# A two-layer trunk in split float32: other steps for the block sums, earlier splits of the x sums, and products of ones while x loads

## The reference, cut to what matters

```python
h = rmsnorm(x, a_norm); proj = h @ a_w_in            # 2048 x 5120
xb, gate = proj[..., :2560], proj[..., 2560:]
xb = causal_depthwise_conv(xb, ...)                  # width 4
y = rg_lru(xb, ...)                                  # two 256-wide block-diagonal products, sigmoid, scan over time
x = x + (y * silu(gate)) @ a_w_out                   # 2560 x 2048
kv = rmsnorm(x, kv_norm) @ w_kv                      # 2048 x 4096: K, then V
q, gate = split(rmsnorm(x, b_norm) @ b_w_in)         # 2048 x 4096
o = stick_breaking_attention(q, k, v)                # 16 heads of 128
x = x + (o * silu(gate)) @ b_w_out
return rmsnorm(x, final_norm)
```

## Time and profile before

| | |
|---|---|
| time, median of 3 runs | 1689.11 us (1686.1, 1689.88, 1689.11) |
| time of the profiled execution | 1688.68 us |
| its span, from the first to the last instruction | 1687.0 us |
| PE busy | 1665.7 us, 99% |
| DVE, ACT, POOL busy | 60%, 49%, 15% |
| DMA queue of SP | 216.16 MB, 41.2% of 16 engines |

### The profile page before, as it was taken

How to read it: one execution, slowest core, us unless ns; L and a number is a source line. 1 busy time by engine, 2 the same in 40 slices (tenths; PEclk the granted TensorE clock), 3 DMA queues, 4 the chain that set the end, 5 groups by cost and what they waited for, 6 DMA issues and landing times.

```text
span 1687.0 us, 24029 instructions
## 1 busy us (share of the span) xinstructions
PE 1665.7 (99%) x7743; PEld 1388.5 (82%) x7743; DVE 1017.3 (60%) x1780; ACT 818.2 (49%) x1626; POOL 260.1 (15%) x251
## 2 busy tenths in 40 slices
PE   8999999999999999999999999999999999999998
PEld 6888888877888888878888888888888888888888
DVE  5787787778774544476664556465655647463333
ACT  6555566655565333355655535444454545432223
POOL 0121211121221313220002111111111111113100
PEclk9999999999999999999999999999999999999999
DMA  5555555665533232346765332323233232323223
GB/s 184 174 180 165 185 168 171 198 196 166 154 95 99 97 97 96 96 146 192 228 189 159 98 100 82 100 81 93 82 105 93 81 100 82 100 76 119 94 94 132
DMA packets 179606, 216.95 MB, mean 129 GB/s; under 512 B 12808, under 2 KB 137944, under 8 KB 179416
## 3 DMA queue, kind: packets, MB, share of 16 engines
q1 hardware_dynamic: 179544, 216.16, 41.2%
HBM read 190.95 MB, written 25.17 MB: 128 GB/s over the span
## 4 chain that ended last, share of the span: by engine, by line
PE 77%; DVE 8%; ACT 5%; DMA 5%; issue 4%; SPq 1%; DVEq 0%; ACTq 0%; POOL 0%; POOLq 0%
PE ps L544 74%; DMA b_raw<-in_w_kv 2%; DVE w_lo L1176 2%; DMA t_scratch<-b_raw 2%; DVE b_raw L1335 1%; PE ps L711 1%; ACT w_hi L817 1%; DVE w_lo L1174 1%; DVE rbuf L1313 1%; ACT w_hi L819 1%; DMA stage<-in_a_w_in 1%; ACT abuf L899 1%; ACT L899 1%; ACT tbuf L896 1%; DVE tbuf L1309 1%
## 5 line engine op out<-in xcount | busy, mean ns | idle before, releaser
L544 PE MATMUL ps<-x_hi,w_hi 128*128 128x512 f32 x1408 | 552.6, 392 | 0.1
L544 PE MATMUL ps<-x_hi,w_lo 128*128 128x512 f32 x1408 | 549.1, 390 | 0.0
L544 PE MATMUL ps<-x_lo,w_hi 128*128 128x512 f32 x1408 | 548.9, 390 | 0.0
L1174 DVE SCALAR_TENSOR_TENSOR w_lo<-stage,cT,w_hi 128x256 fp32r<-128x256 f32 x352 | 206.3, 586 | 329.2 <-ACT w_hi L819 328.8
L817 ACT ACTIVATE w_hi<-stage,cT 128x256 fp32r<-128x256 f32 x352 | 178.4, 507 | 320.1 <-PE ps L544 315.1
L544 PEld LDWEIGHTS ps<-x_hi,w_hi 128*128 128x128 f32 x1408 | 265.0, 188 | 56.9 <-DVE w_lo L1176 3.0
L544 PEld LDWEIGHTS ps<-x_hi,w_lo 128*128 128x128 f32 x1408 | 264.7, 188 | 55.3
L544 PEld LDWEIGHTS ps<-x_lo,w_hi 128*128 128x128 f32 x1408 | 264.9, 188 | 53.6 <-issue 0.2
L1171 DVE TENSOR_TENSOR w_lo<-stage,w_hi 128x512 fp32r<-128x512 f32 x160 | 128.2, 806 | 214.2 <-ACT w_hi L815 214.2
L815 ACT ACTIVATE w_hi<-stage 128x512 fp32r<-128x512 f32 x160 | 100.4, 630 | 279.9 <-PE ps L544 260.0
L819 ACT ACTIVATE w_hi<-stage,cT 128x256 fp32r<-128x256 f32 x352 | 174.4, 496 | 0.0
(11 more groups left out here) (202 smaller groups left out, 2278.8 us busy)
## 6 DMA issues: line engine op xcount, KB each, us to landing
stage<-in_a_w_in SPq DMA_DIRECT2D x160, 256.0 KB, 2.9
stage<-in_b_w_in SPq DMA_DIRECT2D x128, 256.0 KB, 2.8
stage<-in_w_kv SPq DMA_DIRECT2D x95, 256.0 KB, 2.8
stage<-in_a_w_out SPq DMA_DIRECT2D x80, 256.0 KB, 2.6
b_raw<-in_w_kv SPq DMA_DIRECT2D x64, 256.0 KB, 3.5
t_scratch<-b_raw SPq DMA_DIRECT2D x64, 256.0 KB, 3.3
stage<-in_b_w_out SPq DMA_DIRECT2D x64, 256.0 KB, 2.6
stage<-t_scratch SPq DMA_DIRECT2D x45, 256.0 KB, 3.2
```

Of the source, the lines that this page charges most:

```text
L544: mm = pe.matmul(dst, a, b, start=start and n == 0, stop=stop and n == 2, skip_group_check=not check)
L1174: nc.vector.scalar_tensor_tensor(w_lo[:, slot, 0:256], stage[:, slot, 0:256], cT[:, col:col + 1], f(w_hi[:, slot, 0:256]), ALU.mult, ALU.s ...
```

## The change

Three things are changed.

1. **Weight sums.** `b_raw` becomes two sets (c even, c odd), each with its own counters, and the steps change: `T_IN`, `T_OUT` and `T_SUM` are now lists. DVE makes the two groups of an 18-step block at steps 4, 5, 6, 7, 10 and 11, 13, 16, 16, 17.
2. **x sums.** Six of the eight S2 tiles are now split in the last iteration of stage 2. The split of the last two residual tiles (`work2` at position 22) moves behind V step 9 on DVE. POOL makes its last x sums only when DVE has split the operands of 9 V steps, and adds its last squares only after 32.
3. **Start.** PE multiplies `ones` by `ones` (128x128, float32) 4 times before it turns the norm's row, 5 times behind it, and 3 times behind the first transposes. Unit 0 is cut in two: its half with column tile 0 stands ahead of the transposes of tiles 2 and 3, the half with tile 1 behind them. ACT does one small activation on `ones` first, so that its table is loaded before the first weights arrive.

```diff
-S2_HI_AT = {2: 4, 3: 5, 4: 7, 5: 9, 6: 11, 7: 13}
-S3_HI_AT = {i: 8 + 2 * i for i in range(VP)}
+S2_HI_AT = {6: 10, 7: 12}
+S3_HI_AT = {i: 8 + 2 * i if i else 9 for i in range(VP)}
...
-T_IN, T_SUM, T_OUT = 16, 3, 24
+T_IN, T_OUT = (16, 18, 34, 36), (27, 35, 45, 53)
+T_SUM = {4: (0,), 5: (1,), 6: (2,), 7: (3,), 10: (4,), 11: (5,), 13: (6,), 16: (7, 8), 17: (9,)}
...
-                b_raw = sb("b_raw", [P, 4, 512], F32, mem_b)
+                b_raw0 = sb("b_raw0", [P, 4, 512], F32, mem_b)
+                gap("below_b_raw1", 2 * (KR - 4) * 1024, mem_b)
+                b_raw1 = sb("b_raw1", [P, 4, 512], F32, mem_b)
...
-                if not isinstance(it, int) or 4 * it + c:
-                    sp.wait_ge(t_out, it * 256 + 64 * c)
+                if not isinstance(it, int) or 2 * it + c // 2:
+                    sp.wait_ge(t_out[c % 2], it * 128 + 64 * (c // 2))
...
                     for at_j, step in ((T_OUT, sums_out), (T_IN, blocks_in)):
-                        n, e = divmod(9 * c + at_j, N1)
+                        n, e = divmod(at_j[c], N1)
...
+            def spin(times):
+
+                for _ in range(times):
+                    pe.matmul(ps[2][:, 0:P], ones[:, :], ones[:, :], start=True, stop=True)
+
+            pe.wait_ge(id_made, 2)
+            spin(4)
             pe.wait_ge(id_made, 3)
             pe.wait_ge(gain_in, 16)
             turn_rows(rows_g, GAIN_ROWS).then_inc(rows_turned, 1)
+            spin(5)
             turn_x(0)
-            for j in range(8):
+            spin(3)
+            pe.wait_ge(x_lo_ready, 1)
+            unit_t(0, U1, 0, x_hi, x_lo, 0, KD, (0,))
+            turn_x(2)
+            pe.wait_ge(x_lo_ready, 2)
+            unit_t(0, U1, 0, x_hi, x_lo, 0, KD, (1,))
+            for j in range(1, 8):
                 if j < 7:
                     turn_x(2 * j + 2)
...
+            act.wait_ge(id_made, 2)
+            nc.scalar.activation(rb[:, 0:P], ones[:, :], ACT.Identity)
             act.wait_ge(table_ready, 1)
             hi(1, 0, U1)
...
-                    if last and q in (2, 3):
-                        sum_hi(S2, q - 2)
+                    if last and q < 6:
+                        sum_hi(S2, q)
...
-                    if not last and T_SUM <= q % 9 < T_SUM + 5:
-                        block_sum(it, q // 9, q % 9 - T_SUM)
+                    if not last and q % 18 in T_SUM:
+                        for n in T_SUM[q % 18]:
+                            block_sum(it, 2 * (q // 18) + n // 5, n % 5)
...
-                    if last and q in (3, 4):
-                        sum_lo(S2, q - 3)
+                    if last and 1 <= q < 7:
+                        sum_lo(S2, q - 1)
                     if last and LOOK <= q < LOOK + 4:
                         value_step(q - LOOK)
-                    work2(it, q + LOOK)
+                    if not last or q + LOOK != 22:
+                        work2(it, q + LOOK)
...
             for q in range(7, VOPS):
                 value_step(q)
+                if q == 9:
+                    work2(B2 - 1, 22)
...
+            pool.wait_ge(op_lo, 9)
             token_sums(VP - 1)
+            pool.wait_ge(op_lo, 4 * VP)
             squares(VP - 1)
```

More of the change, by code:

```diff
@@ L156, in build @@
             s_lo = sb("s_lo", [P, 4, VP, 256], F32R, mem_s)
-            s2_hi = sb("s2_hi", [P, 2, 256], F32R, mem_s)
+            s2_hi = sb("s2_hi", [P, 6, 256], F32R, mem_s)
         with ExitStack() as mem_r:
@@ L183, in build @@
             with ExitStack() as mem_b:
-                gap("below_b_raw", 2 * (2 * KR - 4) * 1024, mem_b)
-                b_raw = sb("b_raw", [P, 4, 512], F32, mem_b)
+                gap("below_b_raw0", 2 * (KR - 4) * 1024, mem_b)
+                b_raw0 = sb("b_raw0", [P, 4, 512], F32, mem_b)
+                gap("below_b_raw1", 2 * (KR - 4) * 1024, mem_b)
+                b_raw1 = sb("b_raw1", [P, 4, 512], F32, mem_b)
             with ExitStack() as mem_v:
                 v_f = sb("v_f", [P, TT, 1024], F32, mem_v)
-                s_hi = sb("s_hi", [P, 4 * VP - 2, 256], F32R, mem_v)
+                s_hi = sb("s_hi", [P, 4 * VP - 6, 256], F32R, mem_v)
                 v_whi = sb("v_whi", [P, VRING - RING, 512], F32R, mem_v)
@@ L192, in build @@
         u2 = x1
+        b_raw = b_raw0, b_raw1
         with ExitStack() as mem34:
@@ L277, in build @@
         s_lo_ready = [sem(f"s{n + 1}_lo_ready") for n in range(4)]
-        b_in = sem("b_in")
+        b_in = [sem(f"b_in{n}") for n in range(2)]
         t_made = sem("t_made")
-        t_out = sem("t_out")
+        t_out = [sem(f"t_out{n}") for n in range(2)]
         op_full = [sem(f"op_full{n}") for n in range(VRING)]
@@ L343, in s_high @@
             if which == S2:
-                return s2_hi[:, i, :] if i < 2 else s_hi[:, i - 2, :]
-            return s_hi[:, VP - 2 + VP * (S1, S3, S4).index(which) + i, :]
+                return s2_hi[:, i, :] if i < 6 else s_hi[:, i - 6, :]
+            return s_hi[:, VP - 6 + VP * (S1, S3, S4).index(which) + i, :]
         def v_staged(q):
@@ L427, in blocks_in @@
                     src = rows[at(it, 1), row:row + P, col:col + 512].rearrange("n r c -> (n r) c")
-                    sp.dma_start(b_raw[:, n, :], src).then_inc(b_in, 16)
+                    sp.dma_start(b_raw[c % 2][:, n, :], src).then_inc(b_in[c % 2], 16)
             def sums_out(it, c):
@@ L435, in sums_out @@
                     dst = dst[at(it, 1), P * (c // 2):P * (c // 2) + P, 512 * (c % 2):512 * (c % 2) + 512]
-                    sp.dma_start(dst.rearrange("n r c -> (n r) c"), b_raw[:, n, :]).then_inc(t_out, 16)
+                    sp.dma_start(dst.rearrange("n r c -> (n r) c"), b_raw[c % 2][:, n, :]).then_inc(t_out[c % 2], 16)
             def block_sums(it, j, first=False, last=False):
@@ L484, in operand_load @@
                 if q == 0:
-                    sp.wait_ge(t_out, 16 * 4 * VP * VG)
+                    sp.wait_ge(t_out[0], 16 * 4 * VP)
+                    sp.wait_ge(t_out[1], 16 * 4 * VP)
                 if name in ("p1", "p2", "p3"):
@@ L546, in product, with unit_t @@
                 return mm
-            def unit_t(j, u, bank, m_hi, m_lo, k0, k_end):
+            def unit_t(j, u, bank, m_hi, m_lo, k0, k_end, part=(0, 1)):
                 pe.wait_ge(lo_ready, u + 1)
                 s = j % RING
-                for kk in range(2):
+                for kk in part:
                     for m in range(2):
@@ L557, in unit_t @@
                                      k0 + kk == 0, k0 + kk == k_end - 1)
-                mm.then_inc(w_used, 1)
+                if part[-1] == 1:
+                    mm.then_inc(w_used, 1)
             def turn_rows(rows, piece):
@@ L1324, in block_sum @@
                 odd = cT[:, bass.ds(it * 4 + (C_GKV + 2 * (c // 2) + 1), 1)]
-                b11, b12, b22, b21 = (b_raw[:, e, :] for e in range(4))
+                b11, b12, b22, b21 = (b_raw[c % 2][:, e, :] for e in range(4))
                 if n == 0:
-                    dve.wait_ge(b_in, it * 256 + (64 * c + 64))
+                    dve.wait_ge(b_in[c % 2], it * 128 + (64 * (c // 2) + 64))
                     ins = nc.vector.tensor_tensor(b12, b11, b12, ALU.subtract)
```

## The result

| | before | changed |
|---|---|---|
| time, median of 6 runs each | 1688.01 us (1685.81 to 1689.88) | 1702.25 us (1700.92 to 1703.69) |
| ratio, 95% interval | | 1.0086 (1.0073 to 1.0099) |
| span of the profiled execution | 1687.0 us | 1701.5 us |

Predicted were 1678.5 us and a range of 1676 to 1683. The time is 19 us above the range, on the other side of no change. It is the rival that had a chance of 0.03, and 10 us beyond the 1692.5 that was its price.

A forecast was written before the change was run, and what follows sets the result against it. PE is busy nearly throughout, so only its own stops can give time back. Start 2.8, stage 1 5.4 and V products 2.7 sum to 10.9 us, rounded to 10.6: 1689.1 - 10.6 = 1678.5 us, range 1676 to 1683.

The forecast's parts named there:

- SP's queue holds the weights back: Stage 1 rival: weight loads delayed behind SP's wait for sums; 2.1 us lost at each of 7 places, 1692.5 us, chance 0.03.
- the wait goes away: Stage 1: DVE's wait for `b_raw`, 7 times, 25.2 us, vanishes with two sets and the new load steps.
- Landing 5.4 at worst: Term of the queue rival in stage 1: a weight load takes at most 5.4 us to land.
- the 11 that I allowed: Limit in the queue rival: from a load's permission to its use PE has 4 units, 11 us, if DVE has no lead.
- Before, 15 such waits stood in the queue, and PE never waited: Argument against the queue rival: 15 SP waits in the kernel before, with PE never waiting for those loads.
- Stage 1, first kind: PE stops for block-diagonal weights, late because DVE waits for `b_raw`; four stops, 3.4 us, expected to go away.
- Stage 1, second kind: Seven PE stops of 0.29 us, put down to DVE's sums beside the scan; 2.0 us, expected to go away.
- Two at once: Stage 1: two sums together in the step after those beside the scan; one more there, 0.74 us, up to 1.76 beside POOL.
- Start: Kernel's beginning: with products of ones and unit 0 in halves, the third transposes come at 12.9, not 15.80; 2.8 us gained.
- slow until unit 0 is through: Rival at the start: PE's clock stays slow through unit 0, gaining only 0.7 us there; 1680.6 us, chance 0.2.
- the slow end: Lower end for the start: PE stays slow throughout, and 0.7 us is gained.
- V products: Start of the V products: 3.0 us of PE stops vanish, 0.3 comes back at steps 9 to 12; net 2.7 us gained.

The follow-up runs named there:

- e7: Changed kernel with the `b_raw` loads of groups c = 0 and 2 three steps sooner (13 and 31): 1676.5 us, ratio 0.9938.
- e3: Changed kernel with the `b_raw` loads of groups c = 1 and 3 three steps later (21 and 39): 1676.29 us, ratio 0.9932.
- e6: e3 with DVE's weight sums at the steps of the kernel before: 1677.0 us, ratio 0.9939.
- e2: Changed kernel with the old weight sums, steps and single `b_raw`, so only x sums and start changed: 1683.85 us, ratio 0.9976.
- e1: Kernel before with only the weight sums changed, x sums and start as before: 1706.96 us, ratio 1.0111.
- e10: e3 without POOL's two waits, so POOL makes its last x sums and squares at once: 1677.46 us, ratio 0.994.
- e8: e3 without the 12 products of ones: 1677.94 us, ratio 0.9942.
- e4: Changed kernel with the sums of groups c = 1 and 3 sent out two steps sooner (33 and 51): 1676.6 us, ratio 0.9934.

## Why the prediction was wrong

**The step that failed** is the price of the rival "SP's queue holds the weights back", and with it "the wait goes away" in the part on stage 1. DVE's wait for `b_raw` did go away, as predicted. It went to SP, where weights stand behind it. I had named the place, the 7 waits and the sign, and then took each term too small:

- The sums were to land in 3.7 us against a step of 2.7. They took 5.8, because 1 MB of `b_raw` loads had been issued just ahead of them: e7 moves these and gets 3.3. My 3.71 was from a place with no such loads just ahead.
- The delay was to be 1 to 3 us. It was 4.3 in SP's wait, and 1.9 to 2.3 more for the issue of four `b_raw` loads, which I left out. Unit 55's weight was issued 8.0 us behind unit 54's, in e3 2.4: 5.6 us late.
- "Landing 5.4 at worst" was right for unit 55, 5.3; but with 1 MB right ahead that is the usual and not the worst, and unit 54's weight, behind the sums, took 6.0. With these numbers my own sum is 5.6 + 5.3 + 1.9 = 12.8 us, above the 11 that I allowed.
- The limit itself was of the wrong engine. I compared with PE's 11 us for four units, as if ACT and DVE were free. ACT's series from unit 56 to 60 takes 14.2 to 14.9 us in all these kernels, so a weight at its head has to be split 5.2 to 5.8 us ahead of PE, not 1.9.
- So a place cost 3.7 us in place of 2.1, with the stops at units 63 and 65 that follow the one at 60: DVE too, from its low part of 60 to that of 63, takes 8.7 us where PE takes 8.2, and 14.9 to that of 65 where PE takes 13.6. The 2.1 itself stood on no row, and 7 times 2.1 is 3.8 more than 10.9, not 3.4.

"Before, 15 such waits stood in the queue, and PE never waited" was true, and no evidence: there is slack there for the old places (unit 56 split 8.0 us ahead of PE), and the 1 MB stood elsewhere. The trace of before even had the sign, one engine further back. SP's waits, and ACT's for the block-diagonal weight that stands directly behind some of them:

```profile
SPq L428 <- DMA t_scratch<-b_raw: 34.5, 15, 3.0
```

```profile
ACT w_hi L815 <- DMA stage<-in_a_w_i: 19.0, 5, 4.5
```

SP stood 2.3 us in the mean, and ACT waited up to 4.5 us for that weight, which still came in time for PE.

A chance of 0.03 for a mechanism priced within 1 us of its own threshold (10.2 against 11) was the mistake of judgement.

**Stage 1, first kind: right.** With the queue mended (e3), stage 1 loses 1.4 us in place of 7.0, 5.6 gained; predicted 5.4.

**Stage 1, second kind: gone, but for another reason.** I put the 0.29-us stops down to sums beside the scan. e6 has the sums at the old steps and none of those stops. e2, also with the sums at the old steps, has all 7 of them, and DVE's waits for `b_raw` (27.4 us in 7); what e6 changes against it is two sets of `b_raw` and the steps of their loads and write-outs, and DVE's waits are gone. So the stops come with DVE's wait some steps before. That they are its after-effect is the simplest reading; no run separates it from the moved transfers. "Two at once" cost no stop in e3: two took 3.48 us there, over twice 2 x 0.74 and about the 1.76 each of my upper end, and were hidden.

**Start: right, in kind and in size.** Predicted 2.8 us. Up to PE's first matmul behind the norm's spread the changed kernel is 3.5 us ahead of before (42.97 against 46.48), e3 3.8; but these are the two earliest of ten traces. That matmul starts at 42.7 to 44.3 in the ten with the whole new start, 43.4 in the median, and at 45.3 and 46.5 in the two with the old one (e1, before): 2.5 us between the middles. The third transfer of x was estimated to land at 12.9. It landed at 11.64 in the changed kernel's trace and the transposes followed at once, but over the ten it landed at 11.6 to 13.0, though it was issued at 3.34 in every one. The rival "slow until unit 0 is through" fell: in all eleven kernels with the products of ones, and so also in those in which the first x transposes were still slow, PE was fast by 7.9, ahead of unit 0. Timeline of e10's beginning:

```profile
5.73 1.91 PE L579 MATMUL ps<-ident,xraw 128*128 128x128 f32 x8
7.43 0.99 PE L605 MATMUL ps<-ones 128*128 128x128 f32 x6
9.68 1.04 PE L579 MATMUL ps<-ident,xraw 128*128 128x128 f32 x8
```

The Trainium skill, "TensorE: Matmul & The Clock Gate", Part 4, holds that transposes don't count as activity in the way matmuls do; by it I had given the slow end a chance. That end isn't borne out: neither the transposes at 5.67 nor those at 9.23 in the changed kernel put the clock back. The rule itself is left open, since products of ones stood on both sides of them. In e8, with no products of ones and only six matmuls between the first transposes and these, those at 11.26 are still slow. By the medians the ones are worth 1.8 us.

**V products: right.** One stop of 0.86 us in place of 0.23 is left where I had 0.6 lost; PE loses 0.7 us in place of 3.9 in the first 20 us of the V products, some 3.1 gained against 2.7 predicted. Nothing that counts comes back at steps 9 to 12 (0.1 us), since DVE's lead covers it. The stretching itself is there: x_lo's two operations last 2.37 us (1.28 for such a pair undisturbed) and the next 1.22 in place of 0.75. The Trainium skill, "SBUF — State Buffer", "two separate sides", says that the port pair which VectorE and GpSimd share is locked by one of them for a whole instruction. The trace agrees in kind: POOL's instructions last 1.0 us each here, and a wait for one of them allows these 1.1 and 0.5 us. Whether they were priced at 2 us or at nothing decided nothing.

**Together** the intended gains come to 3.8 + 5.6 + 3.1 = 12.5 us in e3's trace (the spans differ by 1687.0 - 1674.0 = 13.0), and by the medians to 1687.93 - 1676.29 = 11.6, some 0.7 of the difference being that trace's early start; 10.9 were predicted. The 26.0 us of stops less 11.6 make 14.4 us slower, and the changed kernel measures 1702.25 - 1688.01 = 14.2.

**What stays open:** ACT's series is 0.6 us longer in the changed kernel (14.85 against 14.26). ACT waits there 0.91 us for DVE's `gate`, in e3 0.25, which is that difference; why DVE is later isn't traced. How the 1 MB slows what is behind it is in part settled: while the sums are on their way, from 154 to 158 us, the 16 DMA engines of the changed kernel are busy all the time (a share of 1.01 and 0.99 in its two halves, 368 and 375 GB/s), so they have no room. Whether the order in the queue adds to that no run shows, since e7 moves both at once.

## What to carry to other kernels

A wait that leaves the waiting engine doesn't vanish; look for the queue that now holds it, and count everything behind it there: the wait, the issue time of what stands between, and the landing beside the bytes just issued. The limit for a late operand is the longest fixed series of any engine between it and PE (here ACT's, and behind it DVE's), not PE's own time for as many units. A rival whose price ends within a microsecond of its threshold deserves a real chance, and the cheapest answer is to leave some steps between a write-out and the load that waits for it, as e3 does: 1676.29 us, the lowest median of all kernels here, though e4 and e7 can't be told from it.

## What the runs showed of the hardware that I had not expected

- Four 256-KB transfers just ahead in SP's queue stretch those behind them: sums out 5.8 us in place of 3.3, a weight 5.3 to 5.6 us in place of the usual 2.8.
- SP's own issue of four transfers takes 1.9 to 2.5 us, in which no weight goes out.
- The place of the same loads decides over many us, at 7 places together: 26 (a wait of 4.3 us ahead of unit 55), then with 2.5 us of wait 18 (unit 56), 13 (unit 57) and 6 (unit 59), and none in e7 (2.1 us, unit 55).
- The rise of TensorE's clock comes at another moment from one execution to the next with the same instructions: behind the same nine products of ones the first eight transposes took 1.1 us in six kernels, 1.39 in two and 1.9 in three. With the landing of the third transfer of x, which moved by 1.4 us, a single profile adds up to 1.6 us of spread to any comparison of starts (42.7 to 44.3 above).
